# Two-layer hybrid decoder on one core: the attention loop's exponentials and weights, by query tile instead of head by head

## The reference

```
def nsa_attention(h, w_qg, w_o, k_cmp, v_cmp, k_slc, v_slc, k_win, v_win):
    ...
        sc = jnp.einsum('bqgrd,bgnd->bgrqn', qb, k_cmp)
        p_c = masked_softmax(sc, cmp_end[None, :] <= tq[:, None])
        o_c = jnp.einsum('bgrqn,bgnd->bqgrd', p_c, v_cmp)
    ...
        ss = jnp.einsum('bqgrd,bgqkld->bgrqkl', qb, ks).reshape(b, G, R, Q_BLOCK, topk * SEL_BLOCK)
        p_s = masked_softmax(ss, m_s).reshape(b, G, R, Q_BLOCK, topk, SEL_BLOCK)
        o_s = jnp.einsum('bgrqkl,bgqkld->bqgrd', p_s, vs)
    ...
        o_w = jnp.einsum('bgrqk,bgkd->bqgrd', masked_softmax(sw, m_w), vw)
        return gb[..., 0:1] * o_c + gb[..., 1:2] * o_s + gb[..., 2:3] * o_w
    ...
    return o @ w_o
```

## Time and profile before

| | |
|---|---|
| three runs | 970.51, 970.57, 972.28 us, median 970.57 |
| the profiled execution | 970.94 us, of which 968.9 us is the span that the trace shows |
| PE busy | 925.4 us (96%) |
| DVE busy | 583.3 us (60%) |
| ACT busy | 519.7 us (54%) |
| granted PE clock | 1.00 over the whole span |
| attention loop, scores of pair 2 to the start of the output projection | 666.87 to 715.80 us |

### The profile page before, as it was taken

The page is one execution under the profiler, slowest core; times in us unless marked ns, Lnnn a source line. Parts: engine busy times, 40 slices in busy tenths (PEclk is TensorE's granted clock), DMA queues, the critical chain, the costliest instruction groups (busy, mean ns, idle before and its releaser), DMA issues.

```text
span 968.9 us, 14299 instructions
## 1 busy us (share of the span) xinstructions
PE 925.4 (96%) x5437; PEld 781.1 (81%) x5437; DVE 583.3 (60%) x965; ACT 519.7 (54%) x919; POOL 23.3 (2%) x47
## 2 busy tenths in 40 slices
PE   5999989999999999999999999998889999999998
PEld 5989978797887877888887788997567788888776
DVE  5767775666566575555544666656857555554465
ACT  6554555766766446444443548245865644444352
POOL 5000000000000000000000000000000000000000
PEclk9999999999999999999999999999999999999999
DMA  9941202021112556777655654420024566565552
GB/s 320 330 138 44 88 0 88 10 78 44 45 45 90 193 166 212 236 232 240 192 175 171 208 186 154 150 88 2 1 89 141 169 191 193 174 191 176 171 187 100
DMA packets 105755, 138.30 MB, mean 143 GB/s; under 512 B 4569, under 2 KB 76514, under 8 KB 105698
## 3 DMA queue, kind: packets, MB, share of 16 engines
q1 hardware_dynamic: 103200, 130.04, 42.0%
q0 software_dynamic: 2160, 7.36, 2.1%
q10 hardware_dynamic: 338, 0.12, 0.0%
HBM read 136.45 MB, written 1.05 MB: 142 GB/s over the span
## 4 chain that ended last, share of the span: by engine, by line
PE 79%; ACT 10%; DVE 8%; issue 2%; ACTq 0%; DMA 0%; SPq 0%; DVEq 0%
PE ps L490 16%; PE ps L492 16%; PE ps L491 16%; PE ps L469 4%; PE ps L474 4%; PE ps L476 4%; PE ps L475 4%; DVE w_lo L1561 3%; ACT w_hi L1098 3%; PE ps L705 3%; PE ps L723 3%; PE ps L938 1%; PE ps L984 1%; ACT qkvT L1495 1%; PE ps L608 1%
## 5 line engine op out<-in xcount | busy, mean ns | idle before, releaser
L1561 DVE TENSOR_TENSOR w_lo<-w_raw,w_hi 128x2048 fp32r<-128x2048 f32 (+2 forms) x100 | 220.7, 2207 | 203.4 <-ACT w_hi L1098 203.3
L1098 ACT ACTIVATE w_hi<-w_raw 128x2048 fp32r<-128x2048 f32 (+2 forms) x100 | 184.4, 1844 | 191.0 <-PE ps L492 150.0
L490 PE MATMUL ps<-w_hi,x_hi 128*128 128x512 f32 x480 | 193.0, 402 | 7.4 <-DVE gdn L1772 2.2
L492 PE MATMUL ps<-w_hi,x_lo 128*128 128x512 f32 x480 | 187.7, 391 | 0.0
L491 PE MATMUL ps<-w_lo,x_hi 128*128 128x512 f32 x480 | 187.2, 390 | 0.0
L490 PEld LDWEIGHTS ps<-w_hi,x_hi 128*128 128x128 f32 x480 | 90.2, 188 | 29.7 <-issue 7.4
L492 PEld LDWEIGHTS ps<-w_hi,x_lo 128*128 128x128 f32 x480 | 90.1, 188 | 19.4
L491 PEld LDWEIGHTS ps<-w_lo,x_hi 128*128 128x128 f32 x480 | 90.3, 188 | 16.8
L474 PE MATMUL ps<-x_hi,w_hi 128*128 128x256 f32 x320 | 92.2, 288 | 0.3 <-DVE w_lo L1607 0.3
L475 PE MATMUL ps<-x_lo,w_hi 128*128 128x256 f32 x320 | 90.9, 284 | 0.0
L490 PE MATMUL ps<-w_hi,big 128*128 128x512 f32 x224 | 89.9, 401 | 1.0 <-DVE w_lo L1561 1.0
(11 more groups left out here) (309 smaller groups left out, 1492.0 us busy)
## 6 DMA issues: line engine op xcount, KB each, us to landing
w_raw<-in_ffn_w_in SPq DMA_DIRECT2D x88, 512.0 KB, 4.5
w_raw<-in_ffn_w_out SPq DMA_DIRECT2D x40, 512.0 KB, 4.1
w_raw<-in_gdn_w_in SPq DMA_DIRECT2D x28, 512.0 KB, 4.8
gdn<-in_gdn_w_in SPq DMA_DIRECT2D x20, 512.0 KB, 8.8
w_raw<-in_gdn_w_out SPq DMA_DIRECT2D x16, 512.0 KB, 4.5
w_raw<-in_ple_w_gate SPq DMA_DIRECT2D x16, 512.0 KB, 4.5
w_raw<-in_kv_w SPq DMA_DIRECT2D x12, 512.0 KB, 4.4
qkvT<-in_cmp_w POOLq DMA_DIRECT2D x8, 512.0 KB, 5.3
```

Of the source, the lines that this page charges most:

```text
L490: mm(o, hi, w_h, start=first and kk == 0, stop=False, skip_group_check=True)
L492: return mm(o, lo, w_h, start=False, stop=end and kk == n - 1, skip_group_check=True)
L1098: A(whi[:, place(stage, q), c0:c0 + n], ring_raw(u) if stage == "qkv" else raw[:, q, 0:n], ACT.Copy).then_inc(S["hi_done"], 1)
L1561: V.tensor_tensor(wlo[:, s, c0:c0 + n], ring_raw(u) if stage == "qkv" else raw[:, q, 0:n], whi[:, s, c0:c0 + n], ALU.subtract).then_inc(S[ ...
```

## The change

On ACT, `exps(p)` does both heads' small exponentials first and then both heads' large ones. On PE, `turned(p, 1)` comes directly behind `turned(p, 0)`, and `scores(p+1, 1)` behind both. On ACT, `wo_quarter` comes ahead of the copies of both heads instead of between them. On DVE, `weights(p, 1)` comes directly behind `weights(p, 0)`, and `out_lo(p-1)` and `wo_quarter` come between the maxima of tile 0 and those of tile 1. No instruction is added or taken away, and what each waits for is the same.

```
@@ PE, loop over p
                     scores(p + 1, 0)
                 turned(p, 0)
+                turned(p, 1)
                 if p < 7:
                     scores(p + 1, 1)
-                turned(p, 1)
                 if p == 1:
                     pe.wait_ge(S["q_sb"], 4)
                     cmp_scores(1, 1)
@@ ACT
             def exps(p):
                 for e in range(2):
-                    i, s1, s0 = 2 * (p % 2) + e, bank(2 + 2 * e, 2, T), bank(3 + 2 * e, 2, P)
+                    i, s0 = 2 * (p % 2) + e, bank(3 + 2 * e, 2, P)
                     act.wait_ge(S["mx0_dve"], 2 * p + e + 1)
                     if p >= 2:
                         act.wait_ge(S["ptr_ps"], 4 * p + 2 * e - 6)
@@
                     last.then_inc(S["p0_act"], 1)
+                for e in range(2):
+                    i, s1 = 2 * (p % 2) + e, bank(2 + 2 * e, 2, T)
                     act.wait_ge(S["mx_dve"], 2 * p + e + 1)
@@ ACT, loop over p
                     out_hi(p - 1)
-                turned(p, 0)
                 for m in ((0,), (1,), (2,), (3,), (4,), (5,), (6, 7))[p - 1]:
                     wo_quarter(m)
+                turned(p, 0)
                 turned(p, 1)
@@ DVE, loop over p
                 weights(p, 0)
+                weights(p, 1)
                 if p < 7:
                     maxima(p + 1, 0, 0)
                     maxima(p + 1, 1, 0)
-                weights(p, 1)
+                out_lo(p - 1)
+                if p >= 3:
+                    wo_quarter(p - 3)
                 if p < 7:
                     maxima(p + 1, 0, 1)
                     maxima(p + 1, 1, 1)
@@
                 if p == 2:
                     cmp_weighted(1)
-                out_lo(p - 1)
-                if p >= 3:
-                    wo_quarter(p - 3)
```

## The result

The changed kernel is slower, and slower than forecast: median 975.68 us over six executions (973.46 to 977.18), against 970.77 us (970.33 to 972.28) for six of the kernel before. The ratio is 1.0041, 95% interval 1.0031 to 1.0051. The forecast was 972.3 with a range up to 974.0. The profiled execution is 975.74 us for a span of 973.6, 4.80 us over the 970.94 of before.

What follows compares the result with a forecast made beforehand. The prediction took a ring of waits across PE, ACT and DVE to bound the attention loop. Its terms, +0.62 +0.60 +1.18 -0.55 -0.41 -0.40 +0.72, sum to +1.76 us on 970.57: 972.3 us, range 970.9 to 974.0.

Steps and rivals of the forecast that it cites:

- The ring of a full turn: Chain of waits across ACT, PE and DVE in the attention loop: 6.25 us, or 6.42 with ACT waiting, against 6.82.
- Turn 3 with cmp_weighted ahead of the weights: From exps(3) to exps(4), DVE's cmp_weighted(1) holds back weights(3,0): 9.33 us laid out, adding 1.18.
- the stall: PE stands idle 2.70 us before output(1), because cmp_shifted is queued behind out_lo(0) on DVE.
- Exps(2): Start of pass 2's exponentials on ACT, laid out 0.62 us later, at 675.85 instead of 675.23.
- Turn 2: From exps(2) to exps(3), with PE idle before output(1): 7.42 us laid out, adding 0.60.
- the end from exps(7) to the projection: Last turn: ACT's two wo_quarters stand ahead of all four copies, delaying the output projection, adding 0.72 us.
- Rival (a): Attention loop: turns 4 to 6 do not shorten and stay at 6.82 us, giving 973.7; chance 0.13.
- (b): PE's wait before output(1) is hidden, cmp_shifted not waiting for out_lo(0), giving 971.2 us; chance 0.13.
- Rival (d): Attention loop: everything overlaps better, five turns of 6.25 us, only 0.62 and 0.72 lost, giving 969.1; chance 0.06.
- rival (c): PE's 2.7 us wait lowers its clock, output(1) and scores(3, tile 0) at half pace, 2.6 us more: 975.0; chance 0.06.
- Theory A: Experiments' theory: PE's 2.54 us wait before output(1) lets the clock fall behind it, on top of the forecast's waits.
- Theory B: Experiments' rival theory: the clock falls are incidental to the change and hit any kernel alike.

Runs made afterwards that it cites:

- e10: The changed kernel run again unaltered, its profile catching an execution without any clock fall: median 975.40 us, ratio 1.0043 to the kernel before.
- e2: The changed kernel with out_lo(0) moved back behind cmp_shifted(1) on DVE: median 971.97 us, ratio 1.0008 to the kernel before.
- e3: The kernel before with only out_lo(0) moved ahead of the tile-1 maxima and cmp_shifted(1): median 973.93 us, ratio 1.0023.
- e8: The changed kernel with the old order restored in four places (p = 1, 2, 3 and 7): median 970.65 us, ratio 0.9994 to the kernel before.
- e7: The changed kernel with PE's scores(p+1, tile 1) back between the two turnings: median 975.81 us, ratio 1.0048 to the kernel before.
- e1: The changed kernel with 22 identity matmuls added on PE between output(0) and output(1), too long a fill: 976.70 us, ratio 1.0053.

## Why the prediction was wrong

**Right.** The ring of a full turn: 6.19 for 6.25 where the maxima are done, 6.44 for 6.42 where ACT waits for them. That wait is there, 0.25 us by these rows of the changed kernel (the last small exponential takes a place of 0.34), laid out as 0.17:

```profile
702.70 0.39 ACT L1495 ACTIVATE qkvT<-ps,head_stats 128x128 f32<-128x128 f32 x1
...
703.29 0.47 ACT L1502 ACTIVATE qkvT<-ps,head_stats 128x256 f32<-128x256 f32 x1
```

Turn 3 with cmp_weighted ahead of the weights, 9.34 for 9.33; the stall, 2.54 for 2.70, and its place. Exps(2) came 0.71 late where 0.62 was laid out (676.09 less the 0.15 by which e10's cmp_turned is late, against 675.23).

**Off in size, at full clock.** Turn 2, 7.62 for 7.42, and the end from exps(7) to the projection, 6.04 for 5.87. With exps(2) these make 0.46 together; the sum was +1.76 and is +2.22. Rival (a), that the turns do not shorten, and (b), that the stall is hidden, did not happen: e10 has turns of 6.19 to 6.45, and e2 shows that the stall has its 1.32 us. Rival (d), that everything overlaps better, fell with the stalls. One sum of the forecast was off by 0.2: a change of +1.2 to +2.8 on 970.57 is 971.8 to 973.4 and not 971.6 to 973.2, so that a little more of it lay over 972.5.

**The step that failed** is the one that dismissed rival (c): "Against it: the wait is half as long, and the 1.04 us in which PE stands in each turn leave the clock at 1.00". Both halves were true of one execution and no ground for a rule. The profile even spoke for (c): at the start PE's matmuls ran at half pace while the view of before printed 1.00, and took their full pace at 16.3 us. The wait of 2.54 us had a fall behind it in two of four profiles and, by the mean clocks, in most executions of the changed kernel; the old wait of 1.64 at 122 us had one in about half of them, in the kernel before as well: 35 of 74 executions at 0.998 or less, none of eleven once it was filled. The one profiled execution of before happened to be among those without a fall while PE worked; that was bad luck, which several executions would have corrected. With the fall taken in, the forecast would have been 972.3 + 0.46 + 1.56 = 974.3; the price of (c), 2.6 us, was too high, because it put all of output(1) and the scores at half pace, and the first 1.3 us behind the stall still ran at full pace (679.17 to 680.5). What is left to 975.7 goes with the fall at 124 us (1.0 to 1.3 us by the medians above), which about half of the executions of before have, and seven of eleven of the changed one if their second fall is that one, as it is in the profile. Whether it is more frequent in the changed kernel, and if so why, stays open: nothing in the change lies ahead of it. The Trainium skill ("TensorE: Matmul & The Clock Gate", Part 1: The HAM clock gate) has PE slowed by default, released by activity, and slowed again by a long enough idle stretch. The half clock behind a stall agrees with that in kind. The Trainium skill speaks there of idle stretches longer than the waits here; the measurement decides, and 2.54 and 1.64 us were enough in some executions and not in others of one program.

Theory A is thus shown for the fall in turn 2, by the fills and by the traces with and without the stall; e3's times agree with it, but its one trace has no fall. Theory B is right in so far as falls occur in any kernel. Not shown is what decides in a given execution; the study has counts only.

## What to carry to other kernels

When an order is changed, look for the first instruction that now waits for another engine's late result, and for who is queued behind it: here one call, out_lo(0), cost 1.3 us by its stall and 1.6 more where the clock fell behind it, and hid a gain in the other turns, 1.0 us of which e8 shows. A PE stall like these two, of 1.6 and 2.5 us, may bring a stretch at half clock behind it: give it a chance of its own, and read the granted clock of several executions before believing that the kernel before has none. A few matmuls of no use in an unavoidable wait of PE are cheap, and the test of whether a wait costs more than itself.

## What was not expected of the hardware

- The clock fell after PE had resumed, not in the stall: 1.3 us behind the 2.54 us wait (679.17 to 680.5) and 1.0 in e7; behind the 1.64 us wait 1.2 us (122.94 to 124.1), and 0.6 to 1.2 over the five traces that have that fall. Each of the nine falls while PE worked lasted 3.4 us.
- Falls also stand behind shorter waits. e1 has a fall at 693.8 after waits of 1.09 and 0.32 us, and e2 one at 717.1 after 0.94 and 0.70, with 0.51 for the clock of 717 to 720. That these waits are the cause is not shown: the same 1.09 and 0.32 stand in e10 with the clock at 1.00. The rows of e2:

```profile
716.64 1.22 PE L469 MATMUL ps<-ident,qkvT 128*128 128x128 f32 x6 [0.70 <-ACT qkvT L1511]
...
717.00:720.00 3.00, 3.00 (x11) 2.51 (x10) 2.41 (x5) 0.98 (x2) 0.00 (x0) 0.51 0.01 3
```

- A 128x128 fp32 matmul of the identity is two records on PE, 0.118 us each (5.18 us for 44 records of 22 calls).
